# Expert layers: later rounds' tokens go through a table in DRAM, and the order of phases is rewritten

## What is computed

```python
def hierarchical_moe(hin, w_group, b_group, w_router, b_router, w_gate, w_up, w_down):
    g_prob = softmax(xf @ w_group + b_group)            # 4 groups
    g_w, g_idx = top_k(g_prob, 1)
    e_logits = (router logits of the chosen group)      # 4 experts in it
    e_val, e_idx = top_k(e_logits, 2)
    gates = one_hot(4 * g_idx + e_idx) * g_w * softmax(e_val)
    for e in range(16):
        hid = silu(xt @ w_gate[e]) * (xt @ w_up[e])     # 1024 -> 512
        y = y + gates[:, e] * (hid @ w_down[e])         # 512 -> 1024
```

## Time and profile before

| | us |
|---|---|
| median of 3 runs | 2656.5 (2654.4 to 2656.8) |
| profiled execution | 2649.1 |
| its span, first to last instruction | 2647.4 |
| PE busy | 2490.9 (94%) |
| DVE busy | 880.9 (33%) |
| ACT busy | 490.8 (19%) |
| POOL busy | 50.8 (2%) |
| expert stage of layer 0: gate 0 starts, combined rows ready | 1851.2, 2153.2 |
| expert stage of layer 1: the same | 2322.5, 2624.2 |

### The profile page before, as it was taken

The page is one execution under the profiler, slowest core; times in us unless marked ns, Lnnn a source line. Parts: engine busy times, 40 slices in busy tenths (PEclk is TensorE's granted clock), DMA queues, the critical chain, the costliest instruction groups (busy, mean ns, idle before and its releaser), DMA issues.

```text
span 2647.4 us, 28337 instructions
## 1 busy us (share of the span) xinstructions
PE 2490.9 (94%) x11282; PEld 1633.5 (62%) x11282; DVE 880.9 (33%) x2172; ACT 490.8 (19%) x1115; POOL 50.8 (2%) x87
## 2 busy tenths in 40 slices
PE   8999999889999999999999999998999979898996
PEld 5688547768854777864777864776433347643332
DVE  1414661461565141455142455233000018310001
ACT  2320002342001222100223100232111112210111
POOL 1000000000000000000000000000000000000000
PEclk9989999989999999999999999998999999999999
DMA  9426544303764332664432654533688893269886
GB/s 352 184 95 261 221 164 153 128 33 127 279 228 161 126 128 96 255 253 159 159 127 96 254 222 159 187 121 140 269 331 325 323 388 112 112 252 399 318 334 254
DMA packets 62723, 548.25 MB, mean 207 GB/s; under 512 B 6649, under 2 KB 9010, under 8 KB 14978
## 3 DMA queue, kind: packets, MB, share of 16 engines
q1 hardware_dynamic: 47232, 470.87, 46.6%
q0 software_dynamic: 12960, 73.27, 7.2%
q10 hardware_dynamic: 2402, 2.30, 0.3%
HBM read 679.55 MB, written 16.49 MB: 263 GB/s over the span
## 4 chain that ended last, share of the span: by engine, by line
PE 80%; DMA 11%; DVE 5%; ACT 2%; issue 1%; SPq 0%; POOL 0%; POOLq 0%; DVEq 0%; ACTq 0%
PE work L452 63%; PE acc L452 15%; DMA weight_ring<-in_stream 4%; DMA ada_ring<-in_ada_stream 2%; DVE att L2357 1%; DMA bias<-in_stream 1%; DMA big<-expert_rows,row_index 1%; PE acc L500 1%; DMA ada_ring<-in_stream 1%; DMA expert_rows<-oT 1%; DMA bias<-bias_copies 1%; DMA bias_copies<-bias_rows 0%; DVE att L2146 0%; DMA bias_rows<-att 0%; ACT att L1421 0%
## 5 line engine op out<-in xcount | busy, mean ns | idle before, releaser
L452 PE MATMUL work<-hT,weight_ring 128*128 128x256 f32 x3264 | 713.9, 380 | 3.7 <-ACT hT L1468 2.2
L452 PEld LDWEIGHTS work<-hT,weight_ring 128*128 128x128 f32 x3264 | 620.7, 191 | 92.1 <-issue 8.2
L452 PE MATMUL work<-weight_ring,hT 128*32 128x512 f32 (+1 forms) x848 | 215.2, 598 | 16.5 <-DMA weight_ring<-in_stream 10.8
L452 PE MATMUL work<-weight_ring,big 128*64 128x512 f32 x704 | 197.4, 611 | 17.9 <-DMA weight_ring<-in_stream 10.4
L452 PE MATMUL work<-weight_ring,att 128*64 128x512 f32 (+2 forms) x656 | 201.1, 596 | 11.2 <-ACT att L1421 11.2
L1421 ACT ACTIVATE big<-work 128x512 f32<-128x512 f32 (+1 forms) x113 | 67.0, 597 | 526.1 <-PE work L452 512.1
L452 PEld LDWEIGHTS work<-weight_ring,hT 128*32 128x32 f32 (+1 forms) x848 | 77.2, 138 | 119.5 <-issue 107.5
L2510 DVE TENSOR_TENSOR big<-work,big 128x512 f32<-128x512 f32 x16 | 11.1, 692 | 404.6 <-PE work L452 404.6
L452 PE MATMUL work<-oT,weight_ring 128*128 128x256 f32 x640 | 145.2, 385 | 0.0
L452 PEld LDWEIGHTS work<-weight_ring,big 128*64 128x64 f32 x704 | 62.2, 140 | 123.8 <-issue 123.8
L2357 DVE SCALAR_TENSOR_TENSOR att<-ada_ring,silu_c,att 128x256 f32<-128x256 f32 x336 | 135.0, 480 | 0.0
(11 more groups left out here) (324 smaller groups left out, 2780.3 us busy)
## 6 DMA issues: line engine op xcount, KB each, us to landing
weight_ring<-in_stream SPq DMA_DIRECT2D x120, 2048.0 KB
weight_ring<-in_stream SPq DMA_DIRECT2D x226, 1024.0 KB, 8.5
ada_ring<-in_stream SPq DMA_DIRECT2D x56, 1024.0 KB
bias<-in_stream SPq DMA_DIRECT2D x56, 1024.0 KB
ada_ring<-in_ada_stream POOLq DMA_DIRECT2D x48, 1024.0 KB, 6.8
expert_rows<-oT POOLq DMA_DIRECT2D x20, 512.0 KB, 8.6
bias_copies<-bias_rows POOLq DMA_DIRECT2D x2, 1536.0 KB, 16.2
ada_ring<-in_stream SPq DMA_DIRECT2D x1, 2048.0 KB
```

What stands on the lines that cost most here:

```text
L452: return pe.matmul(o, a, b, start=start, stop=stop, skip_group_check=True)
```

## The change

Rounds 0 and 1 are gathered as before. For all other rounds POOL scatters the token rows into a DRAM table `token_rows` by four indirect DMAs, once the places are known; ACT loads the 128 rows of a round (0.5 MB) into one of two buffers in `hT`, two rounds ahead; a new step ("lift", p) is eight PE transposes of such a buffer, in two banks. The pick steps and five of the six selections go. The table is cleared once by POOL with eleven writes of 0.5 MB, after its last load of the MLP stages. ACT waits for the scatter ahead of its table load and of SiLU. In `STEPS`, each turn but the last is now followed by some other step than its own down: a lift, a spill round's gate, or another turn. Gate 8 moves ahead of down 1.

```diff
 STEPS = (
-    ("gate", 0), ("up", 0), ("pick", (1, 0)), ("pick", (4, 0)), ("turn", 0), ("down", 0),
-    ("gate", 1), ("up", 1), ("pick", (1, 1)), ("pick", (4, 1)), ("turn", 1), ("down", 1), ("gate", 8),
-    ("gate", 2), ("up", 8), ("up", 2), ("pick", (2, 0)), ("turn", 2), ("down", 2), ("turn", 8), ("down", 8),
-    ("gate", 3), ("up", 3), ("pick", (2, 1)), ("gate", 9), ("turn", 3), ("down", 3),
-    ("gate", 4), ("up", 9), ("up", 4), ("pick", (5, 0)), ("pick", (5, 1)), ("turn", 4), ("down", 4), ("turn", 9), ("down", 9),
-    ("gate", 5), ("pick", (3, 0)), ("up", 5), ("pick", (3, 1)), ("gate", 10), ("turn", 5), ("down", 5),
-    ("gate", 6), ("up", 6), ("up", 10), ("turn", 6), ("down", 6), ("turn", 10), ("down", 10),
+    ("gate", 0), ("up", 0), ("lift", 8), ("turn", 0), ("lift", 2), ("down", 0),
+    ("gate", 1), ("up", 1), ("lift", 3), ("turn", 1), ("gate", 8), ("down", 1),
+    ("gate", 2), ("up", 8), ("up", 2), ("lift", 9), ("turn", 2), ("turn", 8), ("down", 2), ("down", 8),
+    ("gate", 3), ("up", 3), ("lift", 4), ("turn", 3), ("gate", 9), ("down", 3),
+    ("gate", 4), ("up", 9), ("up", 4), ("lift", 5), ("turn", 4), ("turn", 9), ("down", 4), ("down", 9),
+    ("gate", 5), ("lift", 10), ("up", 5), ("lift", 6), ("turn", 5), ("gate", 10), ("down", 5),
+    ("gate", 6), ("up", 6), ("lift", 7), ("up", 10), ("turn", 6), ("turn", 10), ("down", 6), ("down", 10),
     ("gate", 7), ("up", 7), ("spread", 0), ("turn", 7), ("down", 7))
...
+        def waiting(p):
+            return hT[:, (LIFTS.index(p) % 2) * D:(LIFTS.index(p) % 2) * D + D]
...
@@ pe_moe @@
-                    pe.wait_ge(select_ready, layer * DOUBLES + PICKS.index(d) + 1)
-                    for i in range(2):
-                        pe_gather(pe, d, 2 * j + i, u + i)
+                elif kind == "lift":
+                    i = LIFTS.index(n)
+                    pe.wait_ge(tokens_in[i % 2], 16 * (LOADS[i % 2] * layer + i // 2 + 1))
+                    for c in range(2):
+                        pe_open(pe, u + c)
+                        for k in range(4):
+                            ins = pe_transpose(pe, wk(u + c, k * P, k * P + P), waiting(n)[:, (4 * c + k) * P:(4 * c + k) * P + P])
+                        ins.then_inc(work_full, 1)
...
@@ act_moe @@
+            act.wait_ge(tokens_out, 64 * (st.layer + 1))
+
+            def load_tokens(i):
+                act.dma_start(waiting(LIFTS[i]), token_rows[LIFTS[i] * P:LIFTS[i] * P + P]).then_inc(tokens_in[i % 2], 16)
+
+            load_tokens(0)
+            load_tokens(1)
             nc.scalar.preload_act_table_set("silu_and_others")
...
+                elif kind == "lift":
+                    for c in range(2):
+                        act_out(act, u + c, picked(n, 4 * c, 0, 512))
+                    i = LIFTS.index(n) + 2
+                    if i < len(LIFTS):
+                        load_tokens(i)
...
@@ dve_moe @@
+            v.tensor_copy(token_slot[:, :], CM("p")).then_inc(slots_ready, 1)
...
-            selection(1)
-            v.wait_ge(work_full, u0 + 11)
-            selection(4)
-            after = {1: 2, 2: 5, 3: 3}
...
@@ pool_rows @@
+            pool.wait_ge(slots_ready, st.layer + 1)
+            wait_evacuated(pool, range(st.at["unit"] + 2, st.at["unit"] + 6))
+            for tt in range(2):
+                for c in range(2):
+                    pool.indirect_dma_start(token_rows,
+                                            bass.IndirectOffsetOnAxis(ap=token_slot[:, 2 * c + tt:2 * c + tt + 1], axis=0),
+                                            by_token(tt, 0, D), None).then_inc(tokens_out, 16)
@@ POOL's program, after its loop of loads @@
+            zeros = biasT[:, ZEROS:ZEROS + D]
+            pool.wait_ge(acc_full, KB * [st for st in plan if st.kind == "mlp"][-1].at["acc"])
+            pool.memset(zeros, 0.0).then_inc(cleared, 1)
+            pool.wait_ge(cleared, 1)
+            for p in range(ROUNDS):
+                pool.dma_start(token_rows[p * P:p * P + P], zeros).then_inc(zeros_out, 16)
+            pool.wait_ge(zeros_out, 16 * ROUNDS)
```

More of the change, by code:

```diff
@@ L56 @@
 STEPS = (
-    ("gate", 0), ("up", 0), ("pick", (1, 0)), ("pick", (4, 0)), ("turn", 0), ("down", 0),
-    ("gate", 1), ("up", 1), ("pick", (1, 1)), ("pick", (4, 1)), ("turn", 1), ("down", 1), ("gate", 8),
-    ("gate", 2), ("up", 8), ("up", 2), ("pick", (2, 0)), ("turn", 2), ("down", 2), ("turn", 8), ("down", 8),
-    ("gate", 3), ("up", 3), ("pick", (2, 1)), ("gate", 9), ("turn", 3), ("down", 3),
-    ("gate", 4), ("up", 9), ("up", 4), ("pick", (5, 0)), ("pick", (5, 1)), ("turn", 4), ("down", 4), ("turn", 9), ("down", 9),
-    ("gate", 5), ("pick", (3, 0)), ("up", 5), ("pick", (3, 1)), ("gate", 10), ("turn", 5), ("down", 5),
-    ("gate", 6), ("up", 6), ("up", 10), ("turn", 6), ("down", 6), ("turn", 10), ("down", 10),
+    ("gate", 0), ("up", 0), ("lift", 8), ("turn", 0), ("lift", 2), ("down", 0),
[5 more added lines that the diff above has]
+    ("gate", 6), ("up", 6), ("lift", 7), ("up", 10), ("turn", 6), ("turn", 10), ("down", 6), ("down", 10),
     ("gate", 7), ("up", 7), ("spread", 0), ("turn", 7), ("down", 7))
-UNITS = {"gate": 1, "up": 1, "pick": 2, "turn": 1, "spread": 1, "down": 2}
+UNITS = {"gate": 1, "up": 1, "lift": 2, "turn": 1, "spread": 1, "down": 2}
 PHASES = [(n, ("gate", "up", "down").index(kind)) for kind, n in STEPS if kind in ("gate", "up", "down")]
@@ L68 @@
 DOWNS = [n for kind, n in STEPS if kind == "down"]
-PICKS = (0, 1, 4, 2, 5, 3)
+LIFTS = [n for kind, n in STEPS if kind == "lift"]
+GATES = [n for kind, n in STEPS if kind == "gate"]
+assert GATES == [0, 1] + LIFTS
 LAST = DOWNS[-1]
+LOADS = [len(LIFTS[i::2]) for i in range(2)]
 WRITES = (len(DOWNS) - 1) // 2
@@ L142 @@
 ROWS_AT = 1800
+ZEROS = 5200
 class Stage:
@@ L279, in build @@
         copies2 = nc.dram_tensor("bias_copies2", (8, P, ROW), F32, kind="Internal").ap()
+        token_rows = nc.dram_tensor("token_rows", (ROUNDS * P, D), F32, kind="Internal").ap()
         moe_rows = nc.dram_tensor("expert_rows", ((ROUNDS - 1) * P, D), F32, kind="Internal").ap()
         visit_tile = sb("visit_tile", [1, 16], mybir.dt.int32)
+        token_slot = sb("token_slot", [P, 4], mybir.dt.int32)
         row_index = sb("row_index", [P, 4], mybir.dt.int32)
@@ L290, in build @@
         combined = sem("rows_combined")
+        zeros_out = sem("token_rows_cleared")
+        slots_ready = sem("token_slots_ready")
+        tokens_out = sem("token_rows_scattered")
+        tokens_in = [sem(f"token_rows_loaded{i}") for i in range(2)]
+        cleared = sem("zeros_ready")
         tile_begun = sem("tile_begun")
@@ L1252, in by_token, with picked @@
             return big[:, tt * D + a:tt * D + b]
[L1254 to L1257, removed]
+        def picked(p, k, a, b):
+            if p < 2:
+                lo = 8 * S + k * S + p * P
+            else:
+                lo = 8 * S + (GATES.index(p) % 4) * D + k * P
             return big[:, lo + a:lo + b]
+        def waiting(p):
+            return hT[:, (LIFTS.index(p) % 2) * D:(LIFTS.index(p) % 2) * D + D]
         def silu_at(p):
@@ L1273, in weighted, with select @@
             return att[:, 1536 + n * P:1536 + n * P + P]
-        def select(d, tt):
-            lo = 2048 + (PICKS.index(d) % 2) * 512 + tt * S
-            return att[:, lo:lo + S]
+        def select(tt):
+            return att[:, 2048 + tt * S:2048 + tt * S + S]
         def spread_at():
@@ L1287, in row_of, with pe_gather @@
             return (hT, big)[c][:, tt * D:tt * D + D]
-        def pe_gather(pe, d, j, u):
+        def pe_gather(pe, j, u):
             pe_open(pe, u)
@@ L1294, in pe_gather @@
                     k = 2 * j + i
-                    ins = mm(pe, wk(u, i * S, i * S + S), by_token(tt, k * P, k * P + P), select(d, tt), tt == 0, tt == 1)
+                    ins = mm(pe, wk(u, i * S, i * S + S), by_token(tt, k * P, k * P + P), select(tt), tt == 0, tt == 1)
             ins.then_inc(work_full, 1)
@@ L1327, in pe_moe @@
             wait_evacuated(pe, range(u0 + 2, u0 + 6))
-            pe.wait_ge(select_ready, layer * DOUBLES + 1)
+            pe.wait_ge(select_ready, layer + 1)
             for j in range(4):
-                pe_gather(pe, 0, j, u0 + 7 + j)
+                pe_gather(pe, j, u0 + 7 + j)
             def tiles_of(p, w):
@@ L1370, in product @@
                 w = 0 if kind == "gate" else 1
-                d = p // 2
-                if kind == "gate" and p % 2 == 0 and d > 0:
-                    wait_evacuated(pe, [units["pick", (d, j)] + i for j in range(2) for i in range(2)])
+                if kind == "gate" and p in LIFTS:
+                    wait_evacuated(pe, [units["lift", p], units["lift", p] + 1])
                 pe_open(pe, u)
@@ L1377, in product @@
                              for k in range(4 * h, 4 * h + 4)]
-                    ins = several_experts(p, w, h, wk(u), lambda k, a, b: picked(d, k, (p % 2) * P + a, (p % 2) * P + b), steps)
```

(16 more changed lines are left out.)

## The result

The changed kernel takes 2619.45 us (median of 4 runs, 2614.93 to 2629.04); before, four runs beside it have a median of 2655.45 us. The ratio is 0.988, with an interval of 0.984 to 0.992: 31 us faster, between 20 and 42. The profiled execution took 2614.93 us, with a span of 2613.3 us against 2647.4, which is 34.1 us less.

The account below looks back on a forecast made before the run. PE's program order sets the expert stages' pace, the weight stream close behind. Stretch gains of 36.5 us less 0.4 make 36, taking the 2656.5 us median to 2620.5; range 2600 to 2643, 8 in 10.

Parts of the forecast that it names:

- PE's sum: Expert stages, per layer: picks save 35.9 us, lifts cost 9.5, shorter waits save 6.2, turn 10 loses 0.3: 32.3 us.
- The ledger of the bus: Expert stages: bus work is conserved, only its idle time can shrink; waits for weights take back 28 us.
- Forecast gains 12, 8, 7.5, 9: Gains in us for the stretches to up 3 and to up 6, layer 0 and then layer 1.
- The idle that can't go: Bus idle that stays because emptied rings start loads late: 3 us to up 3 in layer 1, 3.9 to up 6.
- The new waits: Weight waits rise to about 15 to 20 us a layer, at gate 2, up 3, gate 4, up 5, gate 6, up 6.
- Rival A: Expert stages: weights aren't the limit, so all 64 us stay, 2592 us; chance 0.12.
- Rival B: Expert stages: the ring mostly forces the bus's idle time, so only 10 us are gained, 2646 us; chance 0.11.
- Rival C: Lifts: the clock halves after transposes, taking 30 of the 36 us, 2651 us; chance 0.05.
- Rival D: Start of the expert stages: tokens come late and PE stops behind up 0; slower, 2670 us; chance 0.06.
- 18 us + 13.2 us: Start of each layer's expert stage: the scatter delay behind 1851.9 above which late tokens decide for slower.
- Rival E: Expert stages: the moved order hides what was hidden, tokens cost what picks cost, 2656 us; chance 0.04.
- Costed at nothing: DVE's selections 0, table clearing 0 (at most 13.7 us), start 0 (up to 5 a layer) plus 0.4 for token slots.

Follow-up runs that it names:

- the light pair: Kernel before and changed kernel, each with base weight loads after a layer's first six tiles halved in bytes; medians 2614.6 and 2544.0 us.
- changed_again: The changed kernel run once more as it is, on the same chip as new_order_2; 2621.1 us, ratio 0.988 to the kernel before.
- light_after: The changed kernel with each base weight load after a layer's first six tiles moving half its bytes; median 2544.0 us.
- new_order_2: The changed kernel with its steps reordered: spill and base phases alternate more evenly, down 6 last before round 7; 2610.5 us against 2621.1.
- scatter_x2: The changed kernel with the token scatter done twice in a row, the second after the first landed; two scatters cost 22.5 us in all.
- The three scatters: The changed kernel with the token scatter done three times in a row; median 2667.9 us, ratio 1.0055 to the kernel before.
- picks_apart: The kernel before with only the step order changed, picks kept and no table; 2642.7 us beside 2653.1, ratio 0.9964.
- lifts_adjacent: The changed kernel with every down directly behind its own turn and gate 8 behind down 1, lifts and table kept; 2620.3 us.

## Why the prediction was right

**Direction and size.** 2620.5 was predicted, 2619.5 measured. The hit to within a microsecond is luck: the parts were off by up to 3 us each, and runs of one kernel spread by 10 to 25.

**PE's sum.** 32.3 us a layer; the light pair shows 33.7. The ten picks, the nine lifts and the waits were each sized from the right row. The waits gave 6.2 us where 5.9 were counted, and PE's busy time, 251.4 and 223.9 us in the light pair, fell by 27.5 where picks less lifts made 26.4.

**The ledger of the bus.** This is the step that made the forecast: removed PE work isn't time, where the weight stream has little idle left. Forecast gains 12, 8, 7.5, 9; measured 12.4, 8.3, 10.1, 7.5. Counted from the DMA packets, layer 1's first stretch kept 2.9 us of idle, just the 3 that I had set aside. The 2.6 us more come from the other half of the rule: the bus's busy time rose by 5.1 us, from 109.2 to 114.3, not by 7.4. The token loads took 7.9, but nearly the same bytes of weights (41.3 MB before, 41.2 after) took 101.0 us instead of 103.8. In the stretch to up 6 two terms were mis-sized and partly cancel. The idle that can't go is 7.1 us in layer 0 and 7.2 in layer 1, where I took 3.9, while the busy time rose by 0.6 and 1.4 instead of 3.7, as 1 to 2 MB of weights fewer fell into the stretch. So the 8 for layer 0 came out by luck, and the 9 for layer 1 was 1.5 too much. The length to up 6 (110 to 112 forecast, 111.2 measured in both layers; 112.8 and 111.5 in changed_again) came out; the DMA share above 0.95 didn't quite, it was 0.94. The new waits stand where they were placed: gate 2 (2.6 us in layer 0, 3.0 in two pieces in layer 1), up 3, gate 4, up 5, up 6. Gate 6 has almost none and gate 3 has some instead.

**Rival A** (all 64 us) falls with the waits, and light_after shows what it would have been. **Rival B** falls with the lengths (111.2 us to up 6, where it had over 116); new_order_2 shows that the ring's order does force a part, some 8 us of the 29.

**Rival C**, half clock behind transposes. In light_after PE's granted clock stays at its 2.4 GHz level for the whole 224 us, through all nine lifts:

```profile
1862.00:2086.00 224.00, 223.13 (x1357) 76.94 (x1360) 6.91 (x10) 33.97 (x59) 4.86 (x9) 1.00 0.66 220
```

Between gate 0 and down 10 of the changed kernel it falls to 1.2 GHz three times a layer, each time behind a wait for weights of over 2 us, as from 1912.57, behind 2.6 us of waiting in gate 2. Lift, turn and lift are 20 transposes in a row, not the 12 that the prediction has. The rule in the Trainium skill, TensorE: Matmul & The Clock Gate, "Part 4: PE-mode transpose", that a transpose does not count as PE work for the clock, shows no cost in runs of up to 20 transposes (2.4 us) that have products right before and behind.

**Rival D** had its mechanism right and its price wrong. The failed step is "18 us + 13.2 us": I took the time until SiLU of gate 0 is wanted as the slack, though lift 8 wants a token load that starts at the same release. In the changed kernel ACT was released at 1853.7 by the landing of the scatter, 21.2 us behind the router's logits (22.9 predicted). Lift 8 started at 1867.0 and the first load took 3.9 us, which leaves 9.5 of slack; with a load of 8.5 us (scatter_x2) 4.9 are left. The three scatters released ACT 31 us a layer, on average, behind the point where it is free in the kernel before. There the prediction had the two kernels level, and this one was 14 us slower. By a straight line between two and three scatters the two kernels are level at about 22 us a layer, an estimate.

**Rival E** (tokens cost what picks cost) falls with the lifts' 1.0 to 1.1 us beside the 3.6 of a pick.

**Costed at nothing, and it was:** DVE's selections and the clearing; the start, costed at 0.4 us in all, didn't get longer (20.6 to 21.1 us from the logits to gate 0 in two profiles, 21.1 before). The tail was costed at 0 with up to 2 us either way and lost 1.4 us a layer. That goes with the order and not with the tokens: picks_apart, with the picks and the new order, has 33.2 and 33.1 us there, lifts_adjacent, with the lifts and the old order, 31.9 and 32.0. What in the order does it is open.

## What to carry to other kernels

Work taken off the engine that sets the order is worth only what the next resource has to spare: make a ledger of that resource for each stretch between two waits for it (busy time is nearly conserved, so idle time is what can shrink), and cap the engine's saving with it. Here it turned 67 us into 38. And ask of an added wait not only when its own engine is needed again, but what is issued behind it and how long that takes once the bus is busy.

## What was not expected of the hardware

Much of the spread of a kernel's times arises early on, where the clock differs, and not in the stage that was changed: of the 6.4 us between the two profiles of the changed kernel, 5.3 are there before the router's logits of layer 0. From 495 us on, the granted clock stays at the 1.2 GHz level for most of 45 us in some executions and for less in others. The first window is of the kernel before, the second of changed_again; the code there is the same:

```profile
495.00:540.00 45.00, 36.01 (x264) 30.14 (x263) 23.41 (x75) 19.23 (x64) 0.00 (x0) 0.89 0.38 141
```

```profile
495.00:540.00 45.00, 38.91 (x194) 34.78 (x194) 13.59 (x38) 12.33 (x37) 0.00 (x0) 0.54 0.25 94
```

Up to 511 us changed_again was some 5 us ahead of the kernel before, and from 543 us on it was 8 us behind, so that it lost about 13 us there; its router's logits come at 1837.7 us instead of 1830.1. Why the clock stays low in one and not in the other is open, and so is whether it is the cause of the loss or goes with it. Stretches counted from a mark in the same profile told kernels apart that medians couldn't.
